# Experts of a hybrid trunk: three of five token tiles from streamed tables, two by fetched rows

## What is computed

```python
q = (x @ peer_wq).reshape(PEER_BLOCK, PEER_HEADS, 2, PEER_HALF)      # 8 heads, two halves of 128
s1 = einsum('nhd,hkd->nhk', q[:, :, 0], peer_k1)                     # 128 keys each
s2 = einsum('nhd,hkd->nhk', q[:, :, 1], peer_k2)
v1, i1 = top_k(s1, 16);  v2, i2 = top_k(s2, 16)
cand = v1[..., :, None] + v2[..., None, :]                           # 256 candidates
cand_idx = i1[..., :, None] * 128 + i2[..., None, :]
best, pos = top_k(cand, 16);  idx = take_along_axis(cand_idx, pos)   # 16 of 16384 experts
g = softmax(best)
act = gelu(einsum('nhkd,nd->nhk', U[idx], x))
return einsum('nhk,nhkd->nd', g * act, V[idx])
```

## Time and profile before

| | |
|---|---|
| median of 3 runs | 5405.83 us (5401.6 to 5411.79) |
| profiled execution, span | 4934.2 us |
| VectorE busy | 3893.0 us, 79% |
| TensorE (matmul) busy | 3129.1 us, 63% |
| GpSimd busy | 2774.2 us, 56% |
| ScalarE busy | 766.9 us, 16% |
| DMA | 1492 MB, of which row fetches 1342 MB |
| mean granted TensorE clock | 0.848 of full speed |

### The profile page before, as it was taken

How to read it: one execution, slowest core, us unless ns; L and a number is a source line. 1 busy time by engine, 2 the same in 40 slices (tenths; PEclk the granted TensorE clock), 3 DMA queues, 4 the chain that set the end, 5 groups by cost and what they waited for, 6 DMA issues and landing times. The chain is left out here.

```text
span 4934.2 us, 39343 instructions
## 1 busy us (share of the span) xinstructions
PE 3129.1 (63%) x11894; PEld 1694.5 (34%) x11894; DVE 3893.0 (79%) x7442; ACT 766.9 (16%) x1900; POOL 2774.2 (56%) x2867
## 2 busy tenths in 40 slices
PE   8989879987055073277978996999713606407137
PEld 3368846542011021023425884754201202102012
DVE  6947665997997997978754766599899799798875
ACT  2112252211010010012111225221100101001001
POOL 0013240767777777766661334066777777777775
PEclk9999969999588597698998996999957958759669
DMA  8700011999999999999993001289999999999998
GB/s 308 233 17 2 4 50 67 367 410 407 410 408 399 409 406 401 409 406 384 417 382 126 2 1 36 78 315 409 409 410 409 400 410 405 407 406 399 410 407 357
DMA packets 434890, 1491.66 MB, mean 302 GB/s; under 512 B 47213, under 2 KB 55525, under 8 KB 433911
## 3 DMA queue, kind: packets, MB, share of 16 engines
q0 software_dynamic: 368640, 1342.34, 68.6%
q1 hardware_dynamic: 66040, 146.81, 8.4%
HBM read 1480.92 MB, written 5.44 MB: 301 GB/s over the span
## 5 line engine op out<-in xcount | busy, mean ns | idle before, releaser
L2072 PE MATMUL ps<-z,o 128*128 128x512 f32 x2356 | 1168.7, 621 | 1541.0 <-DMA z<-in_peer_v,experts 1485.5
L2115 DVE CUSTOM_DVE_ANT_0 z<-z,ps 128x1024 f32<-128x1024 f32 x1176 | 1409.8, 1218 | 69.3 <-DMA z<-in_peer_u,experts 34.4
L1775 POOL DMA_INDIRECT z<-in_peer_u,experts x1176 | 1112.2, 946 | 481.7 <-issue 225.3
L1775 POOL DMA_INDIRECT z<-in_peer_v,experts x1178 | 1131.9, 961 | 425.7 <-issue 281.9
L2072 PEld LDWEIGHTS ps<-z,o 128*128 128x128 f32 x2356 | 410.6, 193 | 2291.5 <-issue 1720.2
L2148 DVE SCALAR_TENSOR_TENSOR ps<-z,state,ps 128x1024 f32<-128x1024 f32 x579 | 745.6, 1288 | 331.1 <-DMA z<-in_peer_v,experts 330.9
L1902 ACT ACTIVATE o<-const,state 128x128 f32<-128x128 f32 x640 | 244.7, 398 | 1139.9 <-PE ps L2072 1087.4
L848 POOL TENSOR_TENSOR kn<-kn,neg_half 128x4 f32<-128x4 f32 x20 | 20.1, 1007 | 341.8 <-DVE kn L891 313.2
L858 POOL TENSOR_TENSOR w<-w,const 128x512 f32<-128x512 f32 x60 | 86.5, 1446 | 209.9 <-DVE w L880 117.8
L463 DVE SCALAR_TENSOR_TENSOR o<-gate,cond,o 128x1024 f32<-128x1024 f32 x160 | 192.5, 1278 | 9.9 <-DMA gate<-in_w_mod 9.7
L858 POOL TENSOR_TENSOR hT<-hT,const 128x512 f32<-128x512 f32 x60 | 85.5, 1430 | 199.5 <-DVE hT L880 103.7
(11 more groups left out here) (443 smaller groups left out, 5265.7 us busy)
## 6 DMA issues: line engine op xcount, KB each, us to landing
gate<-in_w_mod SPq DMA_DIRECT2D x80, 512.0 KB, 4.5
w<-in_w_in SPq DMA_DIRECT2D x12, 2048.0 KB, 10.9
z<-in_peer_v,experts POOLq DMA_INDIRECT x1178, 13.3
z<-in_peer_u,experts POOLq DMA_INDIRECT x1176, 13.4
z<-in_peer_wq SPq DMA_DIRECT2D x4, 2048.0 KB, 15.5
rows<-in_peer_wq SPq DMA_DIRECT2D x4, 2048.0 KB, 16.6
w<-in_peer_wq SPq DMA_DIRECT2D x4, 2048.0 KB, 17.5
rows<-in_w_in SPq DMA_DIRECT2D x3, 2048.0 KB, 18.9
```

The lines of the kernel that those rows point to most:

```text
L1775: eng.indirect_dma_start(slot, None, at_layer_rows(table), bass.IndirectOffsetOnAxis(ap=m.experts[:, t % 2, k:k + 1], axis=0)).then_inc(lo ...
L2072: mm = eng.matmul(m.ps[:, 4 + n, :], m.diag[:, (done + q) % DIAGS, :], row_j[:, n * 512:(n + 1) * 512], start=(q == 0), stop=(q == SLOTS / ...
L2115: eng.tensor_tensor_reduce(row_j, row_j, h_rows, 1.0, 0.0, ALU.mult, ALU.add, m.acts[:, k:k + 1]).then_inc(used_v, 1)
```

## The change

Tiles 0 and 1 still fetch rows. Tiles 2, 3 and 4 (`DENSE`, 384 tokens) don't: for them all 16384 experts are computed, in 128 blocks of 128 experts, block b holding the experts whose first key is b.

* **Gates.** A token's gate for expert (i, j) is the sum of its softmax shares in the slots that chose keys i and j. `rank_step` leaves key numbers and shares of a dense tile in `dense_key` and `dense_share`; TensorE turns them so that slots lie on partitions (`turn_keys`), ScalarE keeps them in `slot_rows`. For each unit of 4 tokens VectorE makes two kinds of one-hot matrices over the keys (`onehots`): four of 128x128, scaled by the share, and one of 128x512. TensorE multiplies them per token (`build_gates`, four products of 128x128), ScalarE writes the result into `gate_chunk` (`keep_build`), and SyncE stores each chunk of 32 tokens (2 MB) to DRAM and later loads groups of 8 blocks (`load_gates`, 1.5 MB). There are 32 units per dense tile.
* **Blocks.** SyncE streams U, turned on the host (`peer_ut`), through 4 buffers and V through 3, 0.5 MB each per block. TensorE makes 8 products of 128x384 (`dense_products`) into a PSUM bank; ScalarE copies and squares them (`keep_block`); VectorE and ScalarE do the GELU, VectorE multiplies with the gates (`dense_block`, `gate_acts`: three operations of 128x384); TensorE adds activations times V into six PSUM banks, 6 products of 512 columns (`dense_sums`). TensorE's order is products(b+1), sums(b).
* **Order.** Tiles are ranked 0, 2, 3, 4, 1. Tile 0's dots are as before, but TensorE adds all 128 of its V rows. Between those from row 54 on stand the 32 units of tile 2. Then come tile 3's units, and with tile 1's dots tile 4's. On VectorE tiles 2, 3 and 4 are ranked in a row, `onehots` behind ranking steps of the tile after. Tile 1's 256 rows are all VectorE's (`dot`, `add_row` into SBUF), and the 128 blocks stand between rows 34 to 252 of them.
* **Smaller.** The ring has 8 buffers, not 13. `late_ring` and `project_ahead` are gone; `stage_norm_project` does all five tiles. `sixteen` becomes `iota` (128 wide).

```diff
-RING, DIAGS = 13, 8
+RING, DIAGS = 8, 8
...
-PROJECTED_AHEAD = TILES - 1
...
-        blocks = [(n, t, min(512, D_IN - n * 512)) for n in range(NB) for t in tiles]
+        blocks = [(n, t, min(512, D_IN - n * 512)) for n in range(NB) for t in range(TILES)]
...
+FETCHED, DENSE = (0, 1), tuple(range(2, TILES))
+RANK_ORDER = (0, 2, 3, 4, 1)
...
+CHUNK, SUB = 32, 4
+CHUNKS, SUBS = NT // CHUNK, P // SUB
+GROUP = 8
...
+def block_behind(b):
+    return 34 + (b * (2 * SLOTS - 36)) // NKEY
...
+    EARLY_BUILD = {54 + 2 * b: b for b in range(SUBS)}
+    BLOCK_BEHIND = {r: [b for b in range(NKEY) if block_behind(b) == r] for r in range(2 * SLOTS)}
...
+                def store_gates(c):
+                    d, last = c * CHUNK // P, (c * CHUNK % P + CHUNK) // SUB - 1
+                    eng.wait_ge(*unit_kept("unit", build_unit(d, last)))
+                    eng.dma_start(m.dense_gates[c], m.gate_chunk[c % 2]).then_inc(gates_stored[c % 2], 16)
...
+                def load_u(b):
+                    if b >= TABLE_U:
+                        eng.wait_ge(*unit_made("unit", block_unit(b - TABLE_U)))
+                    eng.dma_start(m.table_u[b % TABLE_U], m.inp["peer_ut"][l, b]).then_inc(u_loaded[b % TABLE_U], 16)
...
+                for stored in gates_stored:
+                    eng.wait_ge(stored, 16 * CHUNKS // 2)
+                eng.wait_ge(*unit_made("unit", build_unit(ND - 1, SUBS - 1)))
+                load_gates(0)
...
+                def keep_block(b):
+                    u = block_unit(b)
+                    acts = m.ps[:, 6 + u % 2, 0:NT]
+                    if b > 0:
+                        dense_tanh(b - 1)
+                    else:
+                        for stored in gates_stored:
+                            eng.wait_ge(stored, 16 * CHUNKS // 2)
+                    eng.wait_ge(*unit_made("unit", u))
+                    if b >= 2:
+                        eng.wait_ge(v_used, b - 1)
+                    eng.activation(m.dense_acts[b % 2], acts, ACT.Copy).then_inc(acts_kept, 1)
+                    eng.activation(m.dense_inner[b % 2], acts.rearrange("p (d t) -> p d t", d=ND), ACT.Square, scale=0.044715 ** 0.5).then_inc(
+                        unit_kept.sem, unit_kept.one("unit", u))
                 exp_best(0)
...
+                    if k - 4 in EARLY_BUILD:
+                        keep_build(0, EARLY_BUILD[k - 4])
+                exp_best(2)
+                keep_turned(1)
...
+                def build_gates(d, b):
+                    u, n = build_unit(d, b), SUBS * d + b
+                    to = bank_free(u)
+                    eng.wait_ge(second_ready, n + 1)
+                    eng.wait_ge(first_by_vector, n + 1)
+                    for i in range(SUB):
+                        mm = eng.matmul(to[:, i * P:(i + 1) * P], m.second_onehot[n % 2][:, i, :], m.first_onehot[n % 2][:, i, :], start=True, stop=True)
...
+                def dense_products(b):
+                    u = block_unit(b)
+                    to = bank_free(u)
+                    eng.wait_ge(u_loaded[b % TABLE_U], 16 * (b // TABLE_U + 1))
+                    for c in range(KC):
+                        mm = eng.matmul(to[:, 0:NT], m.table_u[b % TABLE_U][:, c, :], m.hT[:, c, D0:TOK], start=(c == 0), stop=(c == KC - 1))
+                    mm.then_inc(unit_made.sem, unit_made.one("unit", u))
...
+                def dense_sums(b):
+                    eng.wait_ge(acts_ready, b + 1)
...
+                    for d in range(ND):
+                        for n in range(2):
+                            mm = eng.matmul(m.ps[:, 2 * d + n, :], m.dense_acts[b % 2][:, d * P:(d + 1) * P], m.table_v[b % TABLE_V][:, n * 512:(n + 1) * 512],
+                                            start=(b == 0), stop=(b == NKEY - 1))
...
+                for k in range(SLOTS):
+                    eng.wait_ge(diags_ready, k + 1)
+                    row_j = row_here(eng, SLOTS + k)
+                    for n in range(2):
+                        mm = eng.matmul(m.ps[:, 4 + n, :], m.diag[:, k % DIAGS, :], row_j[:, n * 512:(n + 1) * 512],
+                                        start=(k == 0), stop=(k == SLOTS - 1))
+                    mm.then_inc(used_t, 1)
+                    if k == 52:
+                        turn_keys(0)
+                    if k in EARLY_BUILD:
+                        build_gates(0, EARLY_BUILD[k])
+                turn_keys(1)
+                for b in range(SUBS):
+                    build_gates(1, b)
+                turn_rows(0)
+                turn_rows(1)
+                turn_keys(2)
+                for b in range(SUBS):
+                    build_gates(2, b)
+                for b in range(NKEY):
+                    dense_products(b)
+                    if b > 0:
+                        dense_sums(b - 1)
+                dense_sums(NKEY - 1)
...
+                def onehots(d, b):
+                    n, at = SUBS * d + b, d * P + b * SUB
+                    if n >= 2:
+                        eng.wait_ge(*unit_made("unit", build_unit((n - 2) // SUBS, (n - 2) % SUBS)))
+                    if b == 0:
+                        eng.wait_ge(*unit_kept("unit", turn_unit(d)))
+                    for i in range(SUB):
+                        ins = eng.tensor_scalar(m.first_onehot[n % 2][:, i, :], const(m, "iota"), m.slot_rows[:, 0, at + i:at + i + 1],
+                                                m.slot_rows[:, 2, at + i:at + i + 1], ALU.is_equal, ALU.mult)
+                    ins.then_inc(first_by_vector, 1)
+                    eng.tensor_tensor(m.second_onehot[n % 2], bc(const(m, "iota"), 1, SUB), bc(m.slot_rows[:, 1, at:at + SUB], 2, NKEY),
+                                      ALU.is_equal).then_inc(second_ready, 1)
...
+                def gate_acts(b):
+                    eng.wait_ge(act_tanh, b + 1)
+                    eng.wait_ge(acts_gated, b + 1)
+                    acts = m.dense_acts[b % 2].rearrange("p (d t) -> p d t", d=ND)
+                    eng.scalar_tensor_tensor(acts, m.dense_inner[b % 2], 1.0, acts, ALU.add, ALU.mult).then_inc(acts_ready, 1)
+                def dense_block(b):
+                    if b > 0:
+                        gate_acts(b - 1)
+                    acts, inner = m.dense_acts[b % 2], m.dense_inner[b % 2]
+                    eng.wait_ge(acts_kept, b + 1)
+                    eng.wait_ge(*unit_kept("unit", block_unit(b)))
+                    eng.scalar_tensor_tensor(inner, inner, 1.0, acts.rearrange("p (d t) -> p d t", d=ND), ALU.add, ALU.mult).then_inc(inner_ready, 1)
+                    eng.wait_ge(inner_ready, b + 1)
+                    if b % GROUP == 0:
+                        eng.wait_ge(gates_loaded[b // GROUP % 2], 16 * (b // GROUP // 2 + 1))
+                    acts = acts.rearrange("p (c t) -> p c t", c=CHUNKS)
+                    eng.tensor_tensor(acts, acts, gate_part(b), ALU.mult).then_inc(acts_gated, 1)
...
+                cube(0, 0)
+                cube(0, 1)
+                weigh(0, 0)
+                rank(1, 0, 4)
+                weigh(0, 1)
+                rank(1, 4, RANK_STEPS)
+                for d in range(ND - 1):
+                    for i in range(RANK_STEPS):
+                        rank(2 + d, i, i + 1)
+                        if i >= 8 and i % 2 == 0 and i < 8 + 2 * SUBS:
+                            onehots(d, (i - 8) // 2)
+                rank(4, 0, HEAD_PAIR_STEPS)
+                for k in range(SLOTS):
+                    dot(1, k)
+                    if k < SUBS:
+                        onehots(2, k)
+                    if k == 6:
+                        eng.wait_ge(used_t, SLOTS)
+                        residual(0, sum_in_banks(4))
+                    if 8 <= k < 18:
+                        rank(4, HEAD_PAIR_STEPS + 2 * (k - 8), HEAD_PAIR_STEPS + 2 * (k - 7))
+                    due, i = spread_steps(k)
+                    if due:
+                        rank(4, i, i + 1)
+                    if 96 <= k < 96 + SHARE_STEPS:
+                        rank(4, RANK_STEPS - SHARE_STEPS + k - 96, RANK_STEPS - SHARE_STEPS + k - 95)
+                    if k == HALF + 2:
+                        cube(1, 0)
+                    if k == 104:
+                        weigh(1, 0)
+                    for b in BLOCK_BEHIND[k]:
+                        dense_block(b)
...
+                for k in range(SLOTS):
+                    if k == LATE_HALF:
+                        weigh(1, 1)
+                    add_row(k)
+                    for b in BLOCK_BEHIND[SLOTS + k]:
+                        dense_block(b)
+                gate_acts(NKEY - 1)
+                eng.wait_ge(used_v, rows_used(NROWS - 1)[0])
+                residual(1, m.row_sum)
+                eng.wait_ge(v_used, NKEY)
+                for d, t in enumerate(DENSE):
+                    residual(t, sum_in_banks(2 * d))
```

516 lines of the change are left out of this document (256 added, 260 removed).

## The result

| | before | changed | ratio |
|---|---|---|---|
| first chip, timed runs | 5403.7 us (5400.3 to 5411.8) | 5791.2 us (5785.5 to 5797.1) | 1.072, interval 1.070 to 1.073 |
| another chip, timed runs | 4936.8 us (4934.2 to 4941.2) | 5761.2 us (5759.7 to 5761.5) | 1.167, interval 1.165 to 1.169 |
| profiled execution, span | 4934.2 us | 5759.7 us (other chip), 5792.4 us (first) | |

The changed kernel is slower, as forecast, but takes 5791 us, not 6230. The forecast **span** was 5757 us. The first profile after spans 5792.4 us and its own time is 5794.2 us: there are no 472 us around a span. The second line is a later run on another chip (run `e8_after_again`), and it is the one that the profile ahead of the prediction fits: its kernel before takes 4937 us. Which chips the first comparison and that profile ran on is not on record.

A forecast was written before the change was run, and what follows sets the result against it. Row fetches were taken to bound the experts stage before, TensorE the blocks after. Layers +326 and +344 and projection +153 gave +823 us on 5406: 6229, said as 6230 us, range 6120 to 6440.

The forecast's parts named there:

- 472 us: Outside the profiled span: 4934 us span against 5406 us median of runs, carried over unchanged into the forecast.
- Rival 3: Time outside the span not fixed: 6307 us if it grows with the span (0.06), 5950 if row fetches (0.06).
- A: Dots of tile 0, first dot to first row product: 207 us, plus 5 for the ring of 8 (bounds 0, +15).
- The sum itself: Stage terms give 2051 us a layer, +326 and +344; with the projection's +153, +823 us in all.
- F: The 128 blocks of a layer, set by TensorE at 10.30 us each: 1318 us and 3 for the start.
- rival 4: TensorE's clock stays at its lower level in the blocks: 20.6 us a block, over 8800 us; chance 0.01.
- term E: Gates' turn through DRAM before the blocks: last chunk out, gates and first U block in; 20 us, bounds 14 and 35.
- Rival 1: Dense matmuls at 429 ns per 512 columns: 5.7 us a block with jitter, time about 5050 us; chance 0.02.
- C: VectorE alone after tile 0's V rows, making tile 3's one-hots (1.5 us a unit) and ranking: 130 us.
- one point of three: Signs of a wrong forecast: block under 7 us, TensorE waiting in the blocks, part outside the span other than 472 us.

The follow-up runs named there:

- e8_after_again: Changed kernel, no edit, run later on another, fast chip beside the kernel before: 5761.2 us, ratio 1.167.
- experiments 1 and 6: 1: kernel before, no edit, run again on a slow chip: 5414.5 us, ratio 0.999. 6: changed kernel, no edit, on a fast chip: 5761.2 us, ratio 1.167.
- experiment 6: Changed kernel, no edit, run on a fast chip beside the kernel before: 5761.2 us, ratio 1.167.
- experiment 5: Changed kernel with the blocks' U, V and activations in bf16 and three fp32 U buffers instead of four: 4484.3 us, ratio 0.908 to the kernel before, fast chip.

## Why the prediction was wrong, and where it was right

**The step that failed** is in its second paragraph: "472 us lie around the first and last instruction". They don't. The span of an execution is its time but for 2 us (5413.2 and 5414.9, 5792.4 and 5794.2). The difference of 472 us was one between two kinds of execution, by all runs one between chips; it sat in the stretches where rows are fetched, and carrying it over unchanged put 6230 in the place of some 5790. The table ahead of the prediction had both numbers, and a timed run 9.6% longer than the span of another execution should have been read as "these are two different executions; what is different?". Rival 3 asked the right question, but split it wrongly twice. It said that nothing in the profile spoke for either side; yet a span that ends with the last instruction of a whole program leaves little room for 472 us. And its price for "belongs to row fetches", -280 us, was by rows fetched (1024 of 2560), where it should have been by what stays on the path. Of the changed kernel's 1024 rows only tile 0's U rows wait for transfers (A, 128 a layer); its V rows go at TensorE's 1.72 us and tile 1's lie beside the blocks.

One could price what is left as 128 x 0.127 us x 2 = 33 us, and 5757 + 33 = 5790 is the measured time. This was worked out with the knowledge of experiments 1 and 6, and its agreement is luck: the later dots are only 6.5 us in each layer, and the late exponential brings 10 more (experiment 6).

**The sum itself held.** Layer 0 took 2051 us (from 862.9 to the last residual's end at 2913.5), layer 1 2052 us, against 1725 and 1707: +326 and +345, forecast +326 and +344. From the last residual of layer 0 to the first dot of layer 1, which holds the projection and the second mixer, 636 us became 790: +153, as forecast, with TensorE's 183 us in it. Span +825.5, forecast +823. On the fast chip the time follows: 4937 + 823 = 5760 us, measured 5761.

Single terms, from the groups of `e8_after_again` (busy us, mean ns):

```profile
L2155 PE MATMUL ps<-hT,z 128*128 128x384 f32 x4096 | 1367.5, 487 | 46.1 <-DMA z<-in_peer_ut 46.1
L2288 DVE TENSOR_SCALAR w<-const,slot_rows 128x128 f32<-128x128 f32 x768 | 223.3, 355 | 98.3 <-PE ps L2140 63.9
L2291 DVE TENSOR_TENSOR z<-const,slot_rows 128x512 f32<-128x512 f32 x192 | 130.9, 682 | 0.0
```

* F, TensorE's price: right, 10.30 forecast, 10.3 measured; granted clock 1.00 throughout, so rival 4 is out. TensorE's whole idle time ahead of its products is 46.1 us, two waits of 23 us for the gates and the first block of U: term E, put at 20.
* Rival 1, half-price products: out. The rows at 858 ns a product decided rightly. The Trainium skill's rate ("Perfetto Trace Analysis", Engine Utilization) makes 427 ns of 128x512, an estimate that agrees with each of a product's two records (429 ns); the prediction held it against the pair. What makes matmuls cheap is the type. In the bf16 kernel of experiment 5, at a granted clock of 1.00, 6 products of 512 columns start 1.31 us ahead of the next list, where 6 fp32 ones took 5.15 us:

```profile
2005.06 1.47 PE L2192 MATMUL ps<-z,hT 128*128 128x512 bf16 x6 [1.06 <-DVE hT L2325]
2006.37 1.46 PE L2181 MATMUL ps<-hT 128*128 128x384 bf16 x8
```

  The Trainium skill ("FP8 and Floating Point Precision", TensorE Precision Notes) lists four passes for true fp32. By that the trace agrees: a quarter of 5.15 us is 1.29 us.
* C, the one-hots: the scalar form took 355 ns queued, not 278, but four and the 512-wide one together took 1.6 us in the timeline (forecast 1.5, bounds 1.2 and 1.9), and C was 124 us where 130 were forecast.
* A, the ring: 212 us where the kernel before has 207, +5 as forecast; eight buffers cost the whole kernel before 27 us on fast chips. On the slow chip A took 228 us; the kernel before took 264 there (861.4 to 1125.7 us in its repeat), so nothing there speaks for a dearer ring.
* What the prediction said would show it wrong came true in one point of three: "a part outside the span other than 472 us".

## What to carry to other kernels

Before a difference between a profile's span and the timed runs is carried over, ask what kind of time it is: here it was another kind of execution, and nearly all of it sat in the stretches where rows are fetched. Price it by what stays on the path there, not by a constant or by bytes. And a ratio is worth as much as its chip: 1.07 on one and 1.17 on another, for the same two kernels, because one waits for fetched rows throughout and the other for TensorE in 1324 of 2051 us of a layer.

## What the hardware showed that I had not expected

* Two kinds of chip: rows fetched evenly at 405 GB/s, or at a mean of 369 GB/s, stopping and going between some 280 and 413 GB/s. Runs on one chip differ by up to 0.5%, the kinds by 9 to 10% in the kernel before. The mixed streams of the bf16 blocks lose 2% (401 against 392 GB/s), neighbouring addresses don't help (5423 us), a shorter ring doesn't change the pace (373 GB/s).
* On a slow chip a signal from TensorE to ScalarE came as much as 42 us after the list it stands behind, while rows were being fetched; on a fast chip the copy began within 0.1 us. The trace of the kernel before holds fewer than half of its semaphore updates there. What in the chip makes it, and whether the recording has a part in it, is open.
* The Trainium skill ("DMA: Bandwidth & Descriptors", Anatomy of one DMA) gives 436 GB/s for the moving part of a transfer, by which a row is estimated at 1.20 us. No run here shows that; 1.28 us apart was the best steady distance of rows, and 1.42 us is the mean of the other kind of chip.
* More rows in flight can go with a longer time: on a slow chip the kernel before took 58 us more with 13 buffers than with 8, on fast chips 27 us less. One run each on the slow side; the difference of 1.1% is over twice what timed runs there scattered (0.4%).
